# The first stage of a hybrid decoder layer: later load of x's second chunk, chunk 0's K tiles between conditioning pairs

## The chip, the cores and the metric

The kernel runs on one core of a Trainium2 chip. The metric is the device time of one execution in microseconds. The profile is of one execution of the same program; its times count from the start of the span, and the execution as a whole took a little longer than its span.

## The reference, cut to what matters

One layer (DEPTH is 1) is computed for 1024 prompt tokens and 8 decode tokens, 1032 columns in all, in float32.

```python
def rmsnorm(x, g):
    xf = x.astype(jnp.float32)
    y = xf * lax.rsqrt(jnp.mean(xf * xf, axis=-1, keepdims=True) + EPS)
    return (y * g).astype(x.dtype)

def layer(x, c, ...):
    mod = jax.nn.silu(c) @ w_ada + b_ada                 # (1024) x (1024, 6144), per sequence
    sh1, sc1, gt1, sh2, sc2, gt2 = jnp.split(mod[:, None, :], 6, axis=-1)
    h = rmsnorm(x, norm1_g) * (1.0 + sc1) + sh1
    proj = h @ w_in
    xr, gr, q, k, v, o, ig, fg, u = jnp.split(proj, _in_splits(), axis=-1)
    ...                                                  # RG-LRU, mLSTM and pool groups -> y_a, y_b, y_c
    x = x + gt1 * (jnp.concatenate([y_a, y_b, y_c], axis=-1) @ w_out)
    h2 = rmsnorm(x, norm2_g) * (1.0 + sc2) + sh2
    x = x + gt2 * (jnp.square(jax.nn.relu(h2 @ w_ff1)) @ w_ff2)
```

Before the first product of `h @ w_in` the kernel needs `sh1` and `sc1`, the first two sixths of `mod`, and the norm of x.

## The kernel before

**Data.** Features lie on partitions (8 K tiles of 128), tokens in the free dimension, in 3 chunks of 344 columns; the decode tokens are the last 8 of chunk 2. Every operand of a dense product is split into a high and a low part of type fp32r, and a product is three matmuls: high x high, low x high, high x low (`dense`). One K tile of one output tile over one chunk is three matmuls of 344 columns.

**The first stage.** SyncE loads x's first chunk, then `w_ada` in 512 KB halves through a ring of four buffers (`RAWW`, `load_raw`). A conditioning *pair* i gives tiles 2i and 2i+1 of `mod`, from two halves; pairs 0 to 3 are `sh1`, pairs 4 to 7 are `sc1`. TensorE multiplies a half in 8 instructions (`ADA:i:0`, `ADA:i:1`), ScalarE copies the result to `ADS` behind the second half, TensorE turns it and adds its four row groups up (`ADT:i`, 4 records in the trace), VectorE writes `MOD` (`ADM:i`; one more step for pairs 4 to 7). `raw_used` makes SyncE wait, before it loads half n, until TensorE has used half n - 4.

**The norm.** For each chunk ScalarE squares 8 K tiles of x and VectorE adds them up (`SQ:c:part`, 4 tiles each), with two buffers between them. TensorE sums over partitions (`NS:c`), ScalarE takes the root, VectorE the reciprocal. A *piece* `N:c:kt` is x times scale times reciprocal on VectorE, the shift, the high part on ScalarE and the low part on GpSimd. The shift is added by ScalarE for K tiles under `SHIFTED` (two passes, `hi_norm`), and by VectorE for the others (`normed`).

**Dense work.** `w_in` is cut into 17 units. Units 0 and 1 are loaded early into `WR` buffers of their own, unit 2 as well; `W:u` splits a unit's weights (high part on ScalarE, low part on GpSimd). `DK:u:c:k0:k1` multiplies K tiles k0 to k1 - 1 of unit u with chunk c, one at a time as pieces become ready; `D:u:c` is the whole product. `WV:j` splits a quarter of `w_v`, `V:t` computes V and the gates of 128 tokens (24 matmuls of 392 columns), which VectorE copies out.

**What sets the order.** The text `MIX_ORDER` is the program: each engine walks through it from the first word to the last and issues what of each word is its own, in that order. `SP_AFTER` says behind which half SyncE issues which other load. Engines meet only at semaphores. PSUM banks are given out by `bank_uses`.

```python
N_SP_RAW = 2 * len(ADA_START) + RAW
SP_AFTER = {3: ("x1",), 10: ("w1", "w0",), 16: ("wv",), 17: ("w2",), 18: ("x2",)}
N_EARLY_W = 3
```

Of the kernel before, what the change touches and what calls it, by code (L numbers as in the profile page):

```python
# [89 lines left out]


MIX_ORDER = """
ADA:0:0 ADA:0:1 SQ:0:0 ADA:4:0 ADA:4:1 SQ:0:1 SQ:1:0 ADT:0 ADM:0 ADA:1:0 SQ:1:1 ADA:1:1 ADT:4 ADM:4 NS:0
ADA:5:0 ADA:5:1 N:0:0 ADT:1 ADM:1 N:0:1 ADA:2:0 ADA:2:1 ADT:5 ADM:5 ADA:6:0 ADA:6:1 ADT:2 ADM:2 N:0:2 ADA:3:0 W:0
    ADA:3:1 ADT:6 N:0:3 W:1 ADM:6 ADA:7:0 ADA:7:1 ADT:3 N:0:4 N:0:5 ADM:3 ADT:7 ADM:7 N:0:6 N:0:7 NS:1
DK:0:0:0:6
WV:0 DK:1:0:0:6
DK:0:0:6:8
WV:1 WV:2 DK:1:0:6:8
ADA:8:0  # L100
D:0:0 WV:3
D:1:0 N:1:0 N:1:1 N:1:2 N:1:3 N:1:4 V:0 SQ:2:0 DK:0:1:0:1
DK:1:1:0:1
DK:0:1:1:2
N:1:5 DK:1:1:1:2
DK:0:1:2:3
N:1:6 N:1:7 DK:1:1:2:3
DK:0:1:3:4
DK:1:1:3:4
SQ:2:1 DK:0:1:4:5  # L110
DK:1:1:4:5
R:20 ADA:8:1 DK:0:1:5:6
V:1 DK:1:1:5:6
NS:2
ADT:8 DK:0:1:6:7
DK:1:1:6:7
DK:0:1:7:8
V:2 DK:1:1:7:8
D:0:1
D:1:1 N:2:8 N:2:0 R:21 N:2:1 N:2:2 N:2:3 N:2:4 N:2:5 N:2:6 V:3 V:4 ADM:8 DK:0:2:0:8  # L120
N:2:7 W:2 V:5
D:0:2 R:22 DK:1:2:0:8
ADA:9:0 ADA:9:1 R:23 V:6 V:7 W:3 V:8 R:25 ADT:9
D:1:2 ADM:9 ADA:10:0 G1 ADA:10:1
# [2758 lines left out]
```

## Time and profile before

| | |
|---|---|
| Median of 3 runs | 1188.4 us (1185.46 to 1189.35) |
| The profiled execution | 1188.24 us |
| Its span | 1186.4 us |
| Mean granted clock of TensorE | 0.986 |
| TensorE, busy | 1126.2 us, 95% of the span |
| VectorE, ScalarE, GpSimd, busy | 795.0, 472.8, 349.9 us |
| DMA | 109.85 MB |

The page's slices show TensorE nearly filled from the third slice on (a slice is 29.7 us); the first two are busy by 4 and 7 tenths, and there the DMA engines are busy by 8. The chain that ended last is 70% TensorE over the whole run. In the timeline a row gives its start, its length, the engine, the line, what is written from what, the count of instructions merged into it, and in brackets the idle time ahead of it with what ended it. A line number is that of the code that records the instruction: L2375 is a conditioning half, L2389 a turn, L2395 a sum of squares, L2404 to L2406 a K tile, L2431 to L2433 V. On VectorE L1760 adds squares, L1739 is the reciprocal, L1725 and L1729 are a piece's first and second instruction, L1714 and L1716 write MOD, L1774 is the low part of w_v. On ScalarE L1251 and L1252 are a piece's two passes, L1297 the eviction ahead of a turn; on GpSimd L1087 is a piece's low part and L1082 that of weights.

### The profile page before, as it was taken

To read this page: it belongs to the slowest core of one execution; us is meant where nothing else is said; L and a number is where in the kernel's file an instruction comes from. 1 tells how busy PE (TensorE), PEld (TensorE's weight loads), DVE (VectorE), ACT (ScalarE), POOL (GpSimd) and SP (SyncE) were. 2 spreads that over 40 slices of the span, in tenths; PEclk is the share of its full clock that TensorE was granted. 3 is DMA by queue.
4 is the path that set the end of the run, shared out by engine and by line. 5 is a ranking of instruction groups with operands and counts; after the bars stand their busy time and mean duration, and the time that the engine had idled before them with its cause. 6 is when DMAs were issued, how large, how long until landed. Compare 5 with 4: busy or idle time off the path is not lost.

```text
span 1186.4 us, 19681 instructions
## 1 busy us (share of the span) xinstructions
PE 1126.2 (95%) x7237; PEld 1075.9 (91%) x7237; DVE 795.0 (67%) x1319; ACT 472.8 (40%) x780; POOL 349.9 (29%) x275
## 2 busy tenths in 40 slices
PE   4799999999989999999999999999999999999997
PEld 2598988798879999899999999999999999999996
DVE  5561455578775434777678778787787787688646
ACT  5551355545456343641332332422432432423431
POOL 0442111101535267763032122122221231231252
PEclk9799999999989999999999999999999999999998
DMA  8812523556623722111111202101201102111104
GB/s 313 309 56 92 152 85 131 182 158 210 189 80 124 267 70 73 50 54 36 37 35 54 71 19 72 53 19 69 71 18 70 54 18 71 53 49 58 36 1 143
DMA packets 67845, 109.85 MB, mean 93 GB/s; under 512 B 6434, under 2 KB 42566, under 8 KB 67398
## 3 DMA queue, kind: packets, MB, share of 16 engines
q1 hardware_dynamic: 57574, 84.88, 21.6%
q10 hardware_dynamic: 10208, 24.12, 6.4%
q8 instruction: 41, 0.67, 0.2%
q14 instruction: 22, 0.18, 0.0%
HBM read 96.81 MB, written 12.18 MB: 92 GB/s over the span
## 4 chain that ended last, share of the span: by engine, by line
PE 70%; DVE 17%; ACT 4%; issue 3%; DMA 2%; POOL 1%; SPq 1%; DVEq 0%; ACTq 0%; POOLq 0%
PE D L2404 7%; PE D L2406 6%; PE D L2405 6%; PE D L2588 5%; PE D L2590 5%; PE D L2589 5%; PE X L2588 4%; PE X L2590 4%; PE X L2589 4%; PE X L2660 4%; PE X L2662 3%; PE X L2661 3%; PE D L2660 2%; PE D L2661 2%; PE D L2662 2%
## 5 line engine op out<-in xcount | busy, mean ns | idle before, releaser
L2404 PE MATMUL D<-H_hi,W_hi 128*128 128x344 f32 x472 | 158.8, 336 | 3.8 <-POOL H_lo L1087 3.1
L2406 PE MATMUL D<-H_hi,W_lo 128*128 128x344 f32 x472 | 152.7, 324 | 0.0
L2405 PE MATMUL D<-H_lo,W_hi 128*128 128x344 f32 x472 | 152.7, 323 | 0.0
L1087 POOL TENSOR_TENSOR Y_lo<-FU,Y_hi 128x344 fp32r<-128x344 f32 (+3 forms) x84 | 105.9, 1263 | 157.7 <-ACT Y_hi L1521 88.6
L1082 POOL TENSOR_TENSOR W_lo<-RAWW,W_hi 128x1024 fp32r<-128x1024 f32 x25 | 61.6, 2466 | 181.7 <-ACT W_hi L1234 181.4
L2404 PEld LDWEIGHTS D<-H_hi,W_hi 128*128 128x128 f32 x472 | 90.8, 192 | 11.9 <-issue 7.6
L1087 POOL TENSOR_TENSOR Y_lo<-EY,Y_hi 128x344 fp32r<-128x344 f32 (+1 forms) x24 | 35.4, 1474 | 220.6 <-ACT Y_hi L1521 143.3
L2405 PEld LDWEIGHTS D<-H_lo,W_hi 128*128 128x128 f32 x472 | 90.5, 192 | 0.9 <-issue 0.5
L2406 PEld LDWEIGHTS D<-H_hi,W_lo 128*128 128x128 f32 x472 | 90.4, 192 | 0.0
L2212 DVE SCALAR_TENSOR_TENSOR X<-X,MOD 128x344 f32<-128x344 f32 (+1 forms) x138 | 75.7, 567 | 9.2 <-PE X L2662 9.0
L2660 PE MATMUL X<-Y_hi,W_hi 128*128 128x344 f32 x252 | 80.7, 320 | 0.0
L2661 PE MATMUL X<-Y_lo,W_hi 128*128 128x344 f32 x252 | 80.6, 320 | 0.0
L2662 PE MATMUL X<-Y_hi,W_lo 128*128 128x344 f32 x252 | 80.5, 319 | 0.0
L2014 DVE SCALAR_TENSOR_TENSOR X<-D,MOD,X 128x344 f32<-128x344 f32 (+1 forms) x72 | 41.3, 573 | 45.4 <-PE D L2590 24.7
L2404 PE MATMUL D<-Y_hi,W_hi 128*128 128x344 f32 x192 | 62.1, 323 | 1.5 <-POOL W_lo L1082 1.5
L1087 POOL TENSOR_TENSOR Y_lo<-KEPT,Y_hi 128x344 fp32r<-128x344 f32 x24 | 26.4, 1099 | 124.1 <-ACT Y_hi L1521 124.1
L1099 POOL TENSOR_TENSOR SS<-SS,SQ 128x344 f32<-128x344 f32 x45 | 43.4, 964 | 65.9 <-ACT SQ L1430 40.4
L2406 PE MATMUL D<-Y_hi,W_lo 128*128 128x344 f32 x192 | 61.3, 320 | 0.0
L2405 PE MATMUL D<-Y_lo,W_hi 128*128 128x344 f32 x192 | 61.3, 319 | 0.0
L1556 ACT ACTIVATE W_hi<-RAWW 128x1024 fp32r<-128x1024 f32 x30 | 31.8, 1059 | 64.2 <-PE X L2662 55.5
L2375 PE MATMUL X<-RAWW,CTX 128*32 128x256 f32 x384 | 35.4, 456 | 19.6 <-DMA RAWW<-in_WADA 19.5
L2212 DVE SCALAR_TENSOR_TENSOR X<-D,MOD,X 128x344 f32<-128x344 f32 (+1 forms) x78 | 42.8, 568 | 16.4 <-PE D L2662 15.4
(416 smaller groups left out, 3443.4 us busy)
## 6 DMA issues: line engine op xcount, KB each, us to landing
RAWW<-in_W SPq DMA_DIRECT2D x76, 512.0 KB, 3.5
RAWW<-in_WADA ACTq DMA_DIRECT2D x28, 512.0 KB, 4.2
RAWW<-in_WADA SPq DMA_DIRECT2D x20, 512.0 KB, 8.0
RAWW<-in_W ACTq DMA_DIRECT2D x18, 512.0 KB, 3.7
X0T<-in_x SPq DMA_DIRECT2D x3, 1376.0 KB, 12.7
out_y<-OUTN SPq DMA_DIRECT2D x24, 172.0 KB
X<-in_x SPq DMA_DIRECT2D x8, 344.0 KB, 4.7
NM<-nm_d SPq DMA_DIRECT2D x8, 256.0 KB, 6.0
```

The source lines that it names most:

```text
L1082: nc.gpsimd.tensor_tensor(lo_v, RAWW[:, raw, :] if src is None else src[:], hi_v.bitcast(F32), ALU.subtract).then_inc(w_lo_ready, 1)
L1087: nc.gpsimd.tensor_tensor(lo_v, fu_v, hi_v.bitcast(F32), ALU.subtract).then_inc(lo_ready, 1)
L2212: V.scalar_tensor_tensor(out=X[:, m, c * CH:c * CH + w], in0=ps[:, 0:w], scalar=MOD[:, 5 * KT + m, 0:1], in1=X[:, m, c * CH:c * CH + w], o ...
L2404: T.matmul(out, w_h, hi[:, kt, a:b], start=(kt == 0), stop=False)
L2405: T.matmul(out, w_h, lo[:, kt, a:b], start=False, stop=False)
L2406: one = T.matmul(out, w_l, hi[:, kt, a:b], start=False, stop=(kt == KT - 1))
L2588: T.matmul(out, w_h, hi(kt), start=(kt == 0 and not onto), stop=False, skip_group_check=onto)
L2589: T.matmul(out, w_h, lo(kt), start=False, stop=False, skip_group_check=onto)
L2590: one = T.matmul(out, w_l, hi(kt), start=False, stop=(kt == n - 1), skip_group_check=onto)
L2660: T.matmul(bank[:, 0:CH], w_hi[:, a:a + P], h, start=(start and k == 0), stop=False, skip_group_check=onto)
L2661: T.matmul(bank[:, 0:CH], w_hi[:, a:a + P], l, start=False, stop=False, skip_group_check=onto)
L2662: one = T.matmul(bank[:, 0:CH], w_lo[:, a:a + P], h, start=False, stop=(stop and k == 1), skip_group_check=onto)
```

## The change

The loads of SyncE are ordered anew, the first seven lines of `MIX_ORDER` are written anew, the low parts of units 0 and 1 are computed on VectorE, and VectorE adds the shift for K tiles 4 to 7 of the first norm. The sum of squares of chunk 1 moves to another bank (X3).

```diff
-SP_AFTER = {3: ("x1",), 10: ("w1", "w0",), 16: ("wv",), 17: ("w2",), 18: ("x2",)}
+SP_AFTER = {7: ("w0", "w1"), 15: ("wv", "x1"), 17: ("x2",), 18: ("w2",)}
 N_EARLY_W = 3
+N_DVE_W = 2
...
-    ADA:3:1 ADT:6 N:0:3 W:1 ADM:6 ADA:7:0 ADA:7:1 ADT:3 N:0:4 N:0:5 ADM:3 ADT:7 ADM:7 N:0:6 N:0:7 NS:1
-DK:0:0:0:6
+ADA:5:0 ADA:5:1 ADT:5 ADM:5 W:0 N:0:2 W:1 N:0:3 ADA:2:0 DK:0:0:0:2 ADA:2:1 DK:1:0:0:2 ADT:2 ADM:2 ADA:6:0 DK:0:0:2:4 ADA:6:1
...
+D:1:0 SQ:1:0 SQ:1:1 V:0 NS:1 ADA:8:0 N:1:0 N:1:1 V:1 N:1:2 N:1:3 DK:0:1:0:1
...
-            add(s, ("X0", "X2", "X0")[s[1]])
+            add(s, ("X0", "X3", "X0")[s[1]])
...
-    SHIFTED = KT - 2
+    SHIFTED, SHIFTED_FIRST = KT - 2, KT // 2
...
-                    if s[1] < N_EARLY_W:
+                    if s[1] < N_DVE_W:
+                        pass
+                    elif s[1] < N_EARLY_W:
                         w_lo(s[1], None, s[1] % 2, WR[s[1]])
...
-                if kt >= SHIFTED:
+                if kt >= (SHIFTED if shift else SHIFTED_FIRST):
                     hi(n, hi_v, fu_v)
...
-                    if kt >= SHIFTED:
+                    if kt >= (SHIFTED if shift else SHIFTED_FIRST):
                         link(one)
                         one = V.tensor_scalar(v, v, MOD[:, shift + kt, 0:1], None, ALU.add)
...
+                elif k == "W" and s[1] < N_DVE_W:
+                    u = s[1]
+                    dve.wait_ge(w_hi_ready, u + 1)
+                    V.tensor_tensor(W_lo[:, u, :], WR[u][:], W_hi[:, u, :].bitcast(F32), ALU.subtract).then_inc(w_lo_ready, 1)
```

`shift` is 0 in the first norm and not 0 in the second, so the second norm keeps its rule.

SyncE's queue at the head, before (x4 and the like are instructions in a row; RAWW is a half, X0T a chunk of x):

```order
L802 DMA X0T_57<-in_x 128x8x344
L556 DMA RAWW_53<-in_WADA 128x2x512 x4
L802 DMA X0T_57<-in_x 128x8x344
L556 DMA RAWW_53<-in_WADA 128x2x512 x7
L822 DMA WR1_86<-in_W 128x1024
L822 DMA WR0_85<-in_W 128x1024
L556 DMA RAWW_53<-in_WADA 128x2x512 x6
L817 DMA WV_raw_97<-in_wv 128x3136
```

The same queue now:

```order
L799 DMA X0T_57<-in_x 128x8x344
L553 DMA RAWW_53<-in_WADA 128x2x512 x8
L819 DMA WR0_85<-in_W 128x1024
L819 DMA WR1_86<-in_W 128x1024
L553 DMA RAWW_53<-in_WADA 128x2x512 x8
L814 DMA WV_raw_97<-in_wv 128x3136
L799 DMA X0T_57<-in_x 128x8x344
```

The second load of x moved from behind four halves to behind all sixteen and w_v; the two units' weights moved forward by three halves.

TensorE behind the pair 1, before (X are conditioning banks, D0 and D1 the dense ones; 2 rows of SEL are a turn):

```order
L2375 MATMUL X4<-RAWW_53,CTX_135 32x256 x8
L2389 MATMUL X1<-SEL_139,ADS_138 128x9 x2
L2375 MATMUL X3<-RAWW_53,CTX_135 32x256 x8
L2389 MATMUL X1<-SEL_139,ADS_138 128x9 x2
L2375 MATMUL X4<-RAWW_53,CTX_135 32x256 x8
L2389 MATMUL X1<-SEL_139,ADS_138 128x9 x4
L2395 MATMUL X2<-SS_124,ONE_142 128x344
L2404 MATMUL D0<-H_hi_49,W_hi_54 128x344
```

TensorE at pair 2 now:

```order
L2378 MATMUL X3<-RAWW_53,CTX_135 32x256 x4
L2407 MATMUL D0<-H_hi_49,W_hi_54 128x344
L2408 MATMUL D0<-H_lo_50,W_hi_54 128x344
L2409 MATMUL D0<-H_hi_49,W_lo_55 128x344
...
L2378 MATMUL X3<-RAWW_53,CTX_135 32x256 x4
L2407 MATMUL D1<-H_hi_49,W_hi_54 128x344
...
L2392 MATMUL X1<-SEL_139,ADS_138 128x9 x2
```

Two K tiles of unit 0 stand between the two halves of pair 2, two of unit 1 between its second half and its turn; pairs 6 and 7 have the like, pair 3 has none.

VectorE around the same place, before:

```order
L1714 TENSOR_TENSOR MOD<-X,COLS 128x18
L1716 SCALAR_TENSOR_TENSOR MOD<-MOD,COLS 128x18
L1714 TENSOR_TENSOR MOD<-X,COLS 128x18
L1725 SCALAR_TENSOR_TENSOR FU<-X0T,MOD,X 128x344 x2
L1714 TENSOR_TENSOR MOD<-X,COLS 128x18
```

VectorE now:

```order
L1715 SCALAR_TENSOR_TENSOR MOD<-MOD,COLS 128x18
L1773 TENSOR_TENSOR W_lo<-WR_85,W_hi 128x1024
L1724 SCALAR_TENSOR_TENSOR FU<-X0T,MOD,X 128x344
L1773 TENSOR_TENSOR W_lo<-WR_86,W_hi 128x1024
L1724 SCALAR_TENSOR_TENSOR FU<-X0T,MOD,X 128x344
L1713 TENSOR_TENSOR MOD<-X,COLS 128x18 x2
```

The low parts of units 0 and 1 stand between the MOD steps of pairs 5 and 2, each ahead of a piece.

## Rows read from the trace of the kernel before

**Rows 1.** Waits: engine and line, releaser, total us, times, longest.

```profile
PE X L2375 <- DMA RAWW<-in_WADA: 19.5, 7, 10.0
```

**Rows 2.** Windows: length, busy us (x) by engine, granted clock, DMA share, GB/s.

```profile
39.00:42.00 3.00, 3.00 (x28) 1.48 (x20) 1.48 (x2) 2.76 (x6) 2.59 (x2) 0.50 0.78 254
...
51.00:54.00 3.00, 3.00 (x21) 3.00 (x21) 2.96 (x4) 0.12 (x1) 0.00 (x0) 1.00 1.07 386
```

**Rows 3.** Timeline of TensorE, 13 to 94 us.

```profile
13.97 1.08 PE L2375 MATMUL X<-RAWW,CTX 128*32 128x256 f32 x8 [0.28 <-DMA RAWW<-in_WADA]
...
24.15 1.94 PE L2375 MATMUL X<-RAWW,CTX 128*32 128x256 f32 x16
...
26.85 1.07 PE L2375 MATMUL X<-RAWW,CTX 128*32 128x256 f32 x16
...
44.05 0.99 PE L2389 MATMUL X<-SEL,ADS 128*128 128x9 f32 x4 [0.77 <-DVE MOD L1714]
44.89 1.50 PE L2395 MATMUL X<-SS,ONE 128*128 128x344 f32 x2
...
48.19 0.49 PE L2405 MATMUL D<-H_lo,W_hi 128*128 128x344 f32 x1
48.48 0.49 PE L2406 MATMUL D<-H_hi,W_lo 128*128 128x344 f32 x1
...
54.30 0.32 PE L2404 MATMUL D<-H_hi,W_hi 128*128 128x344 f32 x1
54.46 0.32 PE L2405 MATMUL D<-H_lo,W_hi 128*128 128x344 f32 x1
...
57.23 0.45 PE L2431 MATMUL X<-WV_hi,H_hi 128*128 128x392 f32 x1 [0.78 <-DVE WV_lo L1774]
...
61.57 0.32 PE L2404 MATMUL D<-H_hi,W_hi 128*128 128x344 f32 x1
...
66.38 0.64 PE L2375 MATMUL X<-RAWW,CTX 128*32 128x256 f32 x8
68.46 0.39 PE L2404 MATMUL D<-H_hi,W_hi 128*128 128x344 f32 x1 [1.43 <-POOL H_lo L1087]
...
93.05 0.42 PE L2404 MATMUL D<-H_hi,W_hi 128*128 128x344 f32 x1 [0.36 <-POOL H_lo L1087]
```

**Rows 4.** SyncE's transfers into RAWW (the first 60 us), then into WR: landing.

```profile
DMA to landing us min/median/max: 3.8/8.0/14.8
...
DMA to landing us min/median/max: 6.1/6.2/11.2
```

**Rows 5.** Groups by line, first 60 us: count, busy us, mean ns, idle before.

```profile
L1087 POOL TENSOR_TENSOR H_lo<-FU,H_hi 128x344 fp32r<-128x344 f32 x10 | 9.3, 940 | 45.1 <-ACT FU L1252 45.1
L1760 DVE TENSOR_TENSOR SS<-SS,SQ 128x344 f32<-128x344 f32 x16 | 8.3, 517 | 8.0 <-ACT SQ L1278 7.4
...
L1725 DVE SCALAR_TENSOR_TENSOR FU<-X0T,MOD,X 128x344 f32<-128x344 f32 x13 | 7.0, 569 | 0.9 <-POOL H_lo L1087 0.7
...
L1251 ACT ACTIVATE H_hi<-FU,MOD 128x344 fp32r<-128x344 f32 x9 | 5.2, 576 | 2.9 <-DVE FU L1725 2.9
...
L1739 DVE RECIPROCAL X<-SS 128x344 f32<-128x344 f32 x2 | 4.6, 2311 | 2.2 <-ACT SS L1257 2.2
...
L1774 DVE TENSOR_TENSOR WV_lo<-WV_raw,WV_hi 128x784 fp32r<-128x784 f32 x4 | 3.7, 972 | 2.2 <-ACT WV_hi L1282 2.2
...
L1297 ACT ACTIVATE ADS<-X 128x256 f32<-128x256 f32 x8 | 3.0, 380 | 15.9 <-PE X L2389 9.9 <-PE X L2375 6.0
```

**Rows 6.** Groups of VectorE over the whole run: splits of a later unit.

```profile
L2031 DVE TENSOR_TENSOR W_lo<-RAWW,W_hi 128x1024 fp32r<-128x1024 f32 x8 | 9.8, 1229 | 12.9 <-ACT W_hi L1234 12.9
```

**Rows 7.** Timelines of VectorE and of GpSimd, 40 to 41 us.

```profile
40.49 0.18 DVE L1714 TENSOR_TENSOR MOD<-X,COLS 128x18 f32<-128x18 f32 x1 [1.80 <-PE X L2389]
40.70 2.02 DVE L1716 SCALAR_TENSOR_TENSOR MOD<-MOD,COLS 128x18 f32<-128x18 f32 x1
...
40.32 2.36 POOL L1082 TENSOR_TENSOR W_lo<-WR,W_hi 128x1024 fp32r<-128x1024 f32 x1
```

More of the change, by code:

```diff
@@ L92 @@
 MIX_ORDER = """
-ADA:0:0 ADA:0:1 SQ:0:0 ADA:4:0 ADA:4:1 SQ:0:1 SQ:1:0 ADT:0 ADM:0 ADA:1:0 SQ:1:1 ADA:1:1 ADT:4 ADM:4 NS:0
-ADA:5:0 ADA:5:1 N:0:0 ADT:1 ADM:1 N:0:1 ADA:2:0 ADA:2:1 ADT:5 ADM:5 ADA:6:0 ADA:6:1 ADT:2 ADM:2 N:0:2 ADA:3:0 W:0
-    ADA:3:1 ADT:6 N:0:3 W:1 ADM:6 ADA:7:0 ADA:7:1 ADT:3 N:0:4 N:0:5 ADM:3 ADT:7 ADM:7 N:0:6 N:0:7 NS:1
-DK:0:0:0:6
[L97 to L100, printed above, removed]
+SQ:0:0 ADA:0:0 SQ:0:1 ADA:0:1 ADA:4:0 ADT:0 ADM:0 NS:0 ADA:4:1 ADT:4 ADM:4 ADA:1:0 N:0:0 ADA:1:1 N:0:1 ADT:1 ADM:1
+ADA:5:0 ADA:5:1 ADT:5 ADM:5 W:0 N:0:2 W:1 N:0:3 ADA:2:0 DK:0:0:0:2 ADA:2:1 DK:1:0:0:2 ADT:2 ADM:2 ADA:6:0 DK:0:0:2:4 ADA:6:1
+    ADT:6 ADM:6 DK:1:0:2:4 N:0:4 ADA:3:0 N:0:5 ADA:3:1 ADT:3 ADM:3 ADA:7:0 DK:0:0:4:6 ADA:7:1 ADT:7 ADM:7 DK:1:0:4:6 N:0:6 N:0:7
+WV:0 WV:1 DK:0:0:6:8
+WV:2 DK:1:0:6:8
 D:0:0 WV:3
-D:1:0 N:1:0 N:1:1 N:1:2 N:1:3 N:1:4 V:0 SQ:2:0 DK:0:1:0:1
+D:1:0 SQ:1:0 SQ:1:1 V:0 NS:1 ADA:8:0 N:1:0 N:1:1 V:1 N:1:2 N:1:3 DK:0:1:0:1
 DK:1:1:0:1
[L104 to L108, printed above, removed]
+N:1:4 DK:0:1:1:2
+DK:1:1:1:2
+N:1:5 DK:0:1:2:3
+DK:1:1:2:3
+N:1:6 DK:0:1:3:4
 DK:1:1:3:4
-SQ:2:1 DK:0:1:4:5
+N:1:7 DK:0:1:4:5
 DK:1:1:4:5
 R:20 ADA:8:1 DK:0:1:5:6
-V:1 DK:1:1:5:6
-NS:2
+SQ:2:0 DK:1:1:5:6
 ADT:8 DK:0:1:6:7
 DK:1:1:6:7
-DK:0:1:7:8
-V:2 DK:1:1:7:8
+SQ:2:1 DK:0:1:7:8
+DK:1:1:7:8
 D:0:1
-D:1:1 N:2:8 N:2:0 R:21 N:2:1 N:2:2 N:2:3 N:2:4 N:2:5 N:2:6 V:3 V:4 ADM:8 DK:0:2:0:8
-N:2:7 W:2 V:5
+D:1:1 V:2 NS:2 N:2:8 N:2:0 R:21 N:2:1 N:2:2 V:3 N:2:3 N:2:4 N:2:5 N:2:6 V:4 ADM:8 N:2:7 DK:0:2:0:8
+W:2 V:5
 D:0:2 R:22 DK:1:2:0:8
```

## The prediction, made before any run of the changed kernel

> **What bounds the kernel now.** I read the waits of TensorE first. Over the whole run its longest wait is for transfers of w_ada: 19.5 us in 7 waits, of which the first is the 10.0 us until any weight has landed [rows 1]. All of it lies before 60 us. TensorE waits little for the rest of the run, so a microsecond won or lost at the head moves everything behind it. I therefore compare the moment at which TensorE has reached the same point of the work.
>
> The windows of the head come next [rows 2]. From 39 to 42 us the granted clock was 0.50, the lower level (1.2 GHz), although TensorE was busy for all of it, with conditioning halves and their turns; from 51 us it was 1.00. The DMA engines moved 386 GB/s from 51 to 54 us, but 254 from 39 to 42: they are not always the bound of the head. The timeline gives the price of a level [rows 3]: dense matmuls follow each other by 0.29 us at the lower clock and by 0.16 at the higher one, so a K tile (three) costs 0.87 or 0.48 us; a conditioning half (8 matmuls) costs 1.08 or 0.64. A turn costs 0.99 at the lower clock, taken as 0.5 at the higher.
>
> The last turn of the sixteen halves ends at 45.0 (44.05 + 0.99); behind chunk 1's sum of squares chunk 0 is multiplied, V of the first 128 tokens starts at 57.23 after a 0.78 us wait, and chunk 1 starts at 61.57; then come waits of 1.43 us at 68.46 and 0.36 at 93.05 [rows 3]. V of 128 tokens costs 4.3 us (61.57 - 57.23), 4.2 of it streaming. The point that I compare is "V:0 and V:1 done, chunk 1 beginning, later waits included": 61.57 + 4.2 + 1.43 + 0.36 = **67.6 us** before.
>
> **The change, part by part.**
>
> *x's second chunk out of the way.* It is 1376 KB. Halves of 512 KB land 1.36 us apart (1.08 of work and 0.28 of waiting at 13.97) [rows 3], so it takes 3.7 us of the stream, and the fifth half can land at 15.3 instead of 19.1. That is no gain by itself: only four halves fit in the ring, and a new one is issued when TensorE has used the one four back. A re-issue into a drained queue lands 3.8 us later at best [rows 4].
>
> *First three pairs.* In the new order pair 0's evicted sums stand on ScalarE behind all eight squares. x lands at about 8.6 (one spacing before the first half at 10.0); eight squares and adds, each add 0.52 and a handover [rows 5], end at 13.4. TensorE: three halves until 13.7, turn to 14.8, sum of squares 1.35 (a start-to-start share of the 1.50 at 44.89) [rows 3] to 16.2, fourth half to 17.3. Each turn now stands directly behind its own pair, so eviction (0.38) [rows 5] and two handovers, 0.46 us, are waited for each time. Turn 18.7, two halves 20.9, 0.7 wait behind the two ScalarE passes of the first K tile, turn 22.5, two halves 24.7, wait and turn **26.1**. The eighth half was re-issued at 17.3 and lands at 21.1 where the bare stream would have brought it at 19.4: 1.7 us of stream lost. Behind it stand w0 and w1. A WR load needed 6.1 us or more to land, against 3.8 for the quickest half [rows 4], though both have 512 KB; bounds are 1.36 us, a half's spacing, and 1.36 + 2.3. I take 2.4 us of stream each, near the middle. The ninth half then lands at 21.1 + 4.8 + 1.36 = 27.3, a wait of 1.1.
>
> *Pairs 2, 6, 3, 7 with ten K tiles between them.* From 27.3 to the last turn there are 8 halves, 4 turns and 10 of the 16 K tiles. At the lower clock: 8.6 + 4.0 + 8.7 = 21.3, plus 2.1 of waits (0.6 for the split of w1, 0.1, three evictions of 0.46) = **50.7**. At the higher clock: 5.1 + 2.0 + 4.8 = 11.9, plus 5.4 of waits (2.3 for w1's split, 0.9 for the third turn's sums queued behind an N piece on ScalarE, 1.3 for a half that could be issued late, two evictions) = **44.5**. So the end of this stretch is no longer set by the DMA stream alone; it depends on TensorE's clock.
>
> *Splits of w0 and w1 on VectorE.* 1.23 us each there [rows 6] instead of 2.36 on GpSimd [rows 7]. They are inside the waits above. Queued behind w1's split is the fourth N piece, behind that the sums of pair 2.
> In the trace the 18-element VectorE step at 40.70 took 2.02 us beside GpSimd's W_lo, begun at 40.32, where the step of the same size ahead of it took 0.18 [rows 7]. The Trainium skill (SBUF — State Buffer, Who interferes with whom) says that a VectorE instruction with two SBUF inputs and a GpSimd instruction that reads SBUF exclude each other and the second waits in full. The trace agrees; by that rule a split on VectorE could wait for one H_lo (0.94) or hold one back, at most 0.9 us more than my sum, which has GpSimd idle when both splits start.
>
> *The shift of K tiles 4 to 7 on VectorE.* A piece cost VectorE one instruction (0.57, of which 0.51 from start to start) and ScalarE two (0.96 from start to start, 0.58 and 0.57 alone) [rows 5]; now VectorE has a second and a handover, about 0.98, and ScalarE 0.49, in each chunk. A K tile of two units is 0.95 us of TensorE, so the pieces just keep up; nothing is won in chunk 0, where pieces wait for sums.
>
> *From the last turn to chunk 1.* Two steps of MOD 0.4, two N pieces 2.0, then ScalarE's first part of w_v (0.85) and four VectorE parts at 0.97 [rows 5], handovers: V:0 starts 7.7 us after the last turn (the six K tiles left fit inside). V:0 4.2, chunk 1's sum 0.8, one half 0.6, V:1 4.2. The squares of chunk 1 (4.4 us, behind w_v's last part on VectorE) end inside V:0; behind the sum stand root 0.55, reciprocal 2.31, the first piece 0.57 + 0.96 + 0.94 [rows 5]: that is 0.75 longer than the half and V:1. Together 7.7 + 4.2 + 0.8 + 0.6 + 4.2 + 0.75 = **18.3**. Later: 0.7 in chunk 1 and 1.3 in chunk 2, whose last pieces now cost VectorE 0.98. My handovers are rounded down; the same count over the rows of before is 0.9 short over this stage, most of it on steps that the new order exposes more often, so I add 0.9.
>
> *Sum.* Lower clock throughout: 50.7 + 18.3 + 2.0 + 0.9 = 71.9, that is +4.3 on 67.6. Higher clock from 27 us: 44.5 + 18.3 + 2.0 + 0.9 = 65.7, that is -1.9. Which one? Before, it went up near 27 us, behind a sum of squares, two halves and a turn without a gap: the 16 matmuls of two halves at 24.15 took 1.94 us, the 16 at 26.85 took 1.07 [rows 3]. It stayed down from 39 to 42 us with halves and turns alone [rows 2], and rose again between 48.48 and 54.30, inside chunk 0's dense matmuls [rows 3]. The new order puts two bursts of 1.7 us between halves at 28 to 34 us, nearer to the case that raised it. I take it as rising after the second burst, which costs 0.6 on top: **-1.3 us**. The profiled execution took 1188.2 us (span 1186.4), the median is 1188.4; so 1187.0 us.
>
> **The rivals.**
> *The clock stays low.* The bursts are too thin among turns and waits, and the ten K tiles cost 0.87 each on a path that was DMA's. For it: 39 to 42 us of before, where a busy TensorE kept 0.50 [rows 2]. Against it: there was no dense work in it. Place: TensorE between 28 and 50 us; it decides against the kernel once the rise comes later than about 40 us (half of the 6.2 us between the two sums). Price +4.3: **1192.6 us**, slower.
> The Trainium skill (TensorE: Matmul & The Clock Gate, What's actually happening) has it that the low clock is the default and activity releases it; by this a mixed stretch can go either way, and the rows above are all that tells here.
>
> *The quick case.* The clock is up from the first sum of squares on: the halves and turns between 17 and 27 us save 1.9 us more, and the new order has no handovers longer than I counted, 0.9. Then -4.1: **1184.2 us**, faster. For it: the first sum of squares now stands closer to halves. Against it: halves still wait for transfers there.
>
> *The stream decides after all.* If w0 and w1 slow the stream more, or the late re-issues add up, the last half comes late and w_v and x's second chunk with it. In my walk the second chunk lands near 48 to 50 us and its squares start near 52 to 58, behind w_v's splits; there are 4 us or more of cover. Above that each microsecond counts in full. I give it little.
>
> **How the numbers follow.** The forecast case, clock rising between 27 and 38 us, 0.55, gives 1185.5 to 1189; low clock 0.2, 1192.6; quick case 0.2, 1184.2; late stream 0.05, above 1190. About 0.3%, 3.6 us, is what a measurement of this kernel tells from no change. The quick case passes that bound in most of its chance, the forecast case in a small part: faster 0.26; slower 0.19 from the low clock and the late stream; same 0.55. The range reaches from a little below the quick case to the low-clock case: 1183.3 to 1192.6.
>
> **What would show it.** Right: the last turn near 45 to 46 us with ten K tiles behind it, dense matmuls before 45 us mostly 0.16 us apart, V:0 7.7 us after the last turn, chunk 1 beginning at 63 to 65 us. Wrong: clock 0.50 until 50 us (low-clock case); the ninth half before 26 us (w0 and w1 cheaper); V:0 waiting for w_v's transfer instead of its splits; a wait of over 1 us at the start of chunk 1 for the second chunk of x; or a difference that arises behind 120 us, where I expect none.

## The result, and the profile after

The changed kernel took 1192.4 us (median of 14 runs, 1188.4 to 1195.7) where the kernel before, on the same chip, took 1187.9 (14 runs): a ratio of 1.0034, with a 95% interval from 1.0020 to 1.0048. It is slower by some 4 us. Eight further runs of the unaltered file gave 1.0020 (1.0000 to 1.0039). The forecast was 1187.0 us; the time is near that of the rival "the clock stays low", 1192.6.

The profiled execution of the changed kernel took 1193.7 us, with a span of 1191.9 and a mean granted clock of 0.983 (before: 1188.2, 1186.4, 0.986). Its windows (length, busy us and count by engine, granted clock, DMA share, GB/s) answer to [rows 2]:

```profile
30.00:33.00 3.00, 2.09 (x15) 1.13 (x14) 1.71 (x2) 1.22 (x3) 0.62 (x1) 1.00 0.58 205
33.00:36.00 3.00, 2.37 (x15) 1.44 (x15) 0.18 (x1) 0.67 (x2) 0.91 (x1) 0.67 0.33 126
36.00:39.00 3.00, 2.44 (x17) 1.58 (x15) 0.00 (x0) 0.38 (x1) 0.00 (x0) 0.76 0.48 175
39.00:42.00 3.00, 2.33 (x25) 1.47 (x24) 2.18 (x6) 0.49 (x1) 0.28 (x1) 1.00 0.79 267
42.00:45.00 3.00, 2.12 (x16) 1.69 (x17) 0.21 (x2) 0.76 (x2) 1.67 (x2) 0.88 1.02 429
45.00:48.00 3.00, 2.44 (x15) 1.19 (x13) 0.00 (x0) 0.38 (x1) 0.00 (x0) 0.50 0.98 363
...
57.00:60.00 3.00, 3.00 (x11) 3.00 (x11) 2.66 (x6) 2.42 (x5) 0.00 (x0) 0.50 1.01 372
60.00:63.00 3.00, 3.00 (x15) 3.00 (x14) 1.09 (x3) 0.52 (x2) 0.00 (x0) 0.78 0.17 51
```

Until 28 us a half still takes 1.08 us, the duration at the lower level, whatever the windows there show (more on this at the end); the clock is high from 30 us, falls between 33 and 39, rises, and falls again near 44; from 45 to 60 us every window has 0.50. Before, it was low from 33.5 to 50.6 us, and its fall came in TensorE's longest wait for a transfer but the first (5.38 us, in the timeline of the kernel before):

```profile
35.28 1.08 PE L2375 MATMUL X<-RAWW,CTX 128*32 128x256 f32 x8 [5.38 <-DMA RAWW<-in_WADA]
```

Behind this half TensorE waited for no transfer any more, so the halves and turns up to 45.0 us ran almost back to back at the lower level, but for 0.77 us of waiting for a step of MOD. What that cost the kernel before is measured in e5.

TensorE's waits of the changed kernel in the first 66 us (engine and line, releaser, total us, times, longest) answer to [rows 1]:

```profile
PE X L2378 <- DMA RAWW<-in_WADA: 11.5, 4, 10.4
PE X L2392 <- ACT ADS L1296: 5.4, 7, 1.5
PE D L2407 <- POOL H_lo L1084: 1.5, 1, 1.5
PE D L2407 <- DVE W_lo L1773: 0.9, 1, 0.9
PE X L2434 <- DVE WV_lo L1777: 0.6, 1, 0.6
```

The wait for transfers fell from 19.5 us to 11.5, and all but 1.1 us of what is left is the first half. In its place stand 5.4 us for ScalarE's evictions of sums, one before almost every turn. TensorE's timeline (start, us, the group, and in brackets the wait ahead of it and its releaser) answers to [rows 3]:

```profile
25.27 1.02 PE L2392 MATMUL X<-SEL,ADS 128*128 128x9 f32 x4 [0.56 <-ACT ADS L1296]
27.00 1.08 PE L2378 MATMUL X<-RAWW,CTX 128*32 128x256 f32 x8 [0.71 <-DMA RAWW<-in_WADA]
...
31.89 0.43 PE L2407 MATMUL D<-H_hi,W_hi 128*128 128x344 f32 x1 [0.91 <-DVE W_lo L1773]
...
45.81 1.08 PE L2378 MATMUL X<-RAWW,CTX 128*32 128x256 f32 x8
47.46 1.03 PE L2392 MATMUL X<-SEL,ADS 128*128 128x9 f32 x4 [0.56 <-ACT ADS L1296]
...
51.86 0.62 PE L2407 MATMUL D<-H_hi,W_hi 128*128 128x344 f32 x1 [1.46 <-POOL H_lo L1084]
...
56.22 0.70 PE L2434 MATMUL X<-WV_hi,H_hi 128*128 128x392 f32 x1 [0.58 <-DVE WV_lo L1777]
56.71 0.53 PE L2435 MATMUL X<-WV_lo,H_hi 128*128 128x392 f32 x1
57.04 0.53 PE L2436 MATMUL X<-WV_hi,H_lo 128*128 128x392 f32 x1
...
62.90 0.74 PE L2398 MATMUL X<-SS,ONE 128*128 128x344 f32 x2
63.56 0.64 PE L2378 MATMUL X<-RAWW,CTX 128*32 128x256 f32 x8
...
69.47 0.39 PE L2407 MATMUL D<-H_hi,W_hi 128*128 128x344 f32 x1 [0.80 <-POOL H_lo L1084]
```

The last turn ends at 48.5 us instead of 45.0, with ten K tiles of chunk 0 already done. V of the first 128 tokens starts at 56.22, a microsecond before it did before, but takes 6.7 us (to 62.90) where it took 4.3: its matmuls follow each other by 0.33 us instead of 0.18.

To compare kernels I take one point that all of them have: VectorE's copy of the last V, of 8 tokens, which ends the first stage. VectorE's timeline of the kernel before, then of the changed one:

```profile
115.82 0.55 DVE L1785 COPY VS<-X 8x384 f32<-8x384 f32 x1 [3.47 <-PE X L2433]
```

```profile
120.11 0.55 DVE L1788 COPY VS<-X 8x384 f32<-8x384 f32 x1 [3.47 <-PE X L2436]
```

That is +4.29 us of the 5.4 between the two profiled times. From this copy to the end of the span the kernel before took 1070.6 us and the changed one 1071.8; in the other profiles here it is 1068.3 to 1071.6, but for e1 (1075.4, taken up at the end). There are short falls of the clock between 235 and 280 us and near 345 that differ from execution to execution. So most of the loss arises before 120 us.

### The profile page after: what moved, and what is told of

It reads as the page before. It is cut to its first block, busy times and chain, and to the rows that moved or that the text cites. A ratio compares the mean times of both kernels' runs of the same rounds, so it can differ in the third digit from the quotient of the medians.

```text
span 1191.9 us, 19690 instructions
## 1 busy us (share of the span) xinstructions
PE 1134.0 (95%) x7237; PEld 1080.9 (91%) x7237; DVE 797.1 (67%) x1327; ACT 470.2 (39%) x774; POOL 345.4 (29%) x273
## 4 chain that ended last, share of the span: by engine, by line
PE 71%; DVE 16%; ACT 4%; issue 3%; DMA 2%; POOL 2%; SPq 1%; DVEq 0%; ACTq 0%; POOLq 0%
PE D L2407 7%; PE D L2409 6%; PE D L2408 6%; PE D L2591 5%; PE D L2593 5%; PE D L2592 5%; PE X L2591 4%; PE X L2593 4%; PE X L2592 4%; PE X L2663 3%; PE X L2665 3%; PE X L2664 3%; PE D L2663 2%; PE D L2664 2%; PE D L2665 2%
## 5 line engine op out<-in xcount | busy, mean ns | idle before, releaser
L2215 DVE SCALAR_TENSOR_TENSOR X<-D,MOD,X 128x344 f32<-128x344 f32 (+1 forms) x78 | 42.8, 568 | 16.4 <-PE D L2665 15.4
L1084 POOL TENSOR_TENSOR H_lo<-FU,H_hi 128x344 fp32r<-128x344 f32 (+2 forms) x33 | 30.4, 936 | 74.6 <-ACT FU L1251 47.6
## 6 DMA issues: line engine op xcount, KB each, us to landing
X0T<-in_x SPq DMA_DIRECT2D x3, 1376.0 KB, 11.5
```

What stands on the lines that cost most here:

```text
L1084: nc.gpsimd.tensor_tensor(lo_v, fu_v, hi_v.bitcast(F32), ALU.subtract).then_inc(lo_ready, 1)
L2215: V.scalar_tensor_tensor(out=X[:, m, c * CH:c * CH + w], in0=ps[:, 0:w], scalar=MOD[:, 5 * KT + m, 0:1], in1=X[:, m, c * CH:c * CH + w], o ...
```

## The experiments

"Stage end" below is the start of that copy, less the 115.82 of before. It comes from one execution of each kernel, and those of e2, e3 and e5 were the shortest of their series; a median is over the whole series. The first half alone starts anywhere from 9.87 to 10.66 us in the profiles named here (9.99 before, 10.37 changed, 9.95 in e1), so a few tenths between two stage ends say nothing. "F:n" is n matmuls of 128x344 into a bank that nobody reads; they fill waits of TensorE and do no other work.

**e1: the changed kernel with its waits filled.**

```
-  ... ADA:2:0 DK:0:0:0:2 ADA:2:1 DK:1:0:0:2 ADT:2 ... ADA:6:1
-      ADT:6 ... ADA:3:1 ADT:3 ... ADA:7:1 ADT:7 ...
-  WV:0 WV:1 DK:0:0:6:8
-  D:1:0 SQ:1:0 SQ:1:1 V:0 ...
+  ... ADA:2:0 DK:0:0:0:2 ADA:2:1 F:5 DK:1:0:0:2 F:3 ADT:2 ... ADA:6:1
+      F:3 ADT:6 ... ADA:3:1 F:8 ADT:3 ... ADA:7:1 F:3 ADT:7 ...
+  WV:0 WV:1 F:8 DK:0:0:6:8
+  D:1:0 SQ:1:0 SQ:1:1 F:3 V:0 ...
```

> The changed kernel with 33 extra matmuls of 344 columns into a bank that is still unused, put where TensorE waited between 31 and 56 us (5 and 3 around pair 2's tiles, 3 before turn 6, 8 before turn 3, 3 before turn 7, 8 before K tile 6, 3 before V:0); all results stay as they are. Theory C (the clock): the changed order leaves TensorE with too many waits, the clock falls at 44 us and stays low until 61, in V:0 too. Then these matmuls keep it up: V:0 takes 4.3 us instead of 6.7, chunk 1 begins at 64 to 66 us instead of 69.5, and the time is 3 to 5 us under the changed kernel's, about that of the kernel before. Theory L (the chain of latencies): the loss is that each turn waits for its own pair's eviction and that ring buffers are issued late; the last turn then stays at 48 us, and with 33 extra matmuls the time is the changed kernel's or up to 2 us more.

Measured: 1189.4 us (12 runs), ratio 1.0002 (0.9985 to 1.0019), 3 us less than the changed kernel; the two intervals, this and 1.0020 to 1.0048, don't overlap, though this one does overlap that of the repeated changed kernel (1.0000 to 1.0039). TensorE's timeline, then a window:

```profile
44.60 0.61 PE L2392 MATMUL X<-SEL,ADS 128*128 128x9 f32 x4
...
52.87 0.45 PE L2434 MATMUL X<-WV_hi,H_hi 128*128 128x392 f32 x1 [1.33 <-DVE WV_lo L1777]
...
53.50 0.34 PE L2434 MATMUL X<-WV_hi,H_hi 128*128 128x392 f32 x1
```

```profile
45.00:48.00 3.00, 2.52 (x16) 2.23 (x16) 2.21 (x6) 0.79 (x2) 0.64 (x1) 1.00 1.09 397
```

The windows from 33 to 66 us all have a granted clock of 1.00, and the halves from 34.0 us on take 0.64 us each. The last turn ends at 45.2 instead of 48.5, V's matmuls follow by 0.18 us again, and the stage end is at -1.06. Work that computes nothing, 33 matmuls of it, brought the stage end 5.35 us forward. The order, the transfers and the splits are those of the changed kernel, and 0.42 us is the earlier first half; what is left is, as far as these traces show, the clock's. Against the second profile of the unaltered kernel (e11, below), in which the clock stayed up for longer, the same work brought 2.2 us: what fillers are worth depends on the course that they are compared with. The stage end is also where the forecast's sum for a clock that rises and stays had put it, -1.3.

**e2: the changed kernel with the ten K tiles behind the last turn again.**

```
-  (DK:0:0:0:2 DK:1:0:0:2 DK:0:0:2:4 DK:1:0:2:4 DK:0:0:4:6 DK:1:0:4:6 from among halves and turns)
-  WV:0 WV:1 DK:0:0:6:8
+  DK:0:0:0:6 DK:1:0:0:6 WV:0 WV:1 DK:0:0:6:8
```

> The changed kernel, but the K tiles of chunk 0 are all multiplied behind the last turn, as before the change; loads, turns, splits and V as in the changed kernel. Theory C: the last turn comes some 4 us earlier than 48.5, since 10 K tiles at mostly the lower clock are gone from ahead of it; then 12 K tiles in a row raise the clock before V:0, which takes 4.3 us; chunk 1 begins at 65 to 67 us, the time is 1 to 3 us under the changed kernel's. Theory L: the last turn gains what the tiles cost, but the tiles cost it again behind; time as the changed kernel within 1 us.

Measured: 1191.9 us (12 runs), ratio 1.0034 (1.0021 to 1.0048); stage end +1.26. In the median it is no better than the changed kernel, so K tiles among halves are not by themselves what costs. The profiled execution, the shortest of the twelve (1189.5), ends the stage 3 us before the changed kernel's first profile and level with its second: all sixteen K tiles stand together, the clock rises among them near 47.5 us, and V:0 takes 4.5 us. The loss has another source as well, which shows without the tiles:

```profile
32.31 1.02 PE L2390 MATMUL X<-SEL,ADS 128*128 128x9 f32 x4 [4.72 <-ACT ADS L1294]
...
35.76 1.02 PE L2390 MATMUL X<-SEL,ADS 128*128 128x9 f32 x4 [0.56 <-ACT ADS L1294]
...
40.38 1.03 PE L2390 MATMUL X<-SEL,ADS 128*128 128x9 f32 x4 [1.73 <-ACT ADS L1294]
```

TensorE waits 4.72 us for the sums of pair 2, which are queued on ScalarE behind the splits of w0 and w1 and two N pieces. All the evictions together cost it 10.9 us in the first 66. The last turn ends at 44.9, where before's ended (45.0): what the late second chunk of x gave to the stream, the turns behind their own pairs took. All of this ran at the lower level: from 21.4 us to the last turn every two halves took 1.94 us and every turn 1.02. Only from 13.7 to 18.3 us was the clock up here, with 0.64 us for a half.

**e3: the order of pairs, turns and K tiles of before; only x's second chunk late, with what follows from it.**

```
   (of the changed kernel)
-  SQ:0:0 ADA:0:0 SQ:0:1 ADA:0:1 ADA:4:0 ADT:0 ADM:0 NS:0 ... (its first stage up to DK:1:0:6:8)
+  ADA:0:0 ADA:0:1 SQ:0:0 ADA:4:0 ADA:4:1 SQ:0:1 ADT:0 ... (that of before, without SQ:1:0, SQ:1:1, NS:1)
```

> One part alone: x's second chunk late, w_v and the two units' weights as in the changed kernel, and all words of chunk 1 and of V as there; but pairs, turns, pieces and K tiles of chunk 0 in the order of the kernel before. Both theories: last turn near 43 to 45 us. Theory C: TensorE has the dense stretch of before, V:0 at the higher clock, chunk 1 begins at 66 to 67.5, the time within 1.5 us of the kernel before. If the late chunk itself is the cost (theory X: its squares and reciprocal stand behind V:0 and are waited for), the time is 3 us or more over the kernel before whatever the clock.

Measured: 1188.9 us (12 runs), ratio 1.0011 (0.9997 to 1.0026), last turn at 42.8, chunk 1 beginning at 64.6, stage end -0.59. So the load moved back, V of 256 tokens moved ahead, the splits on VectorE and the four shifts make no difference that is measured. The last turn does come 2.3 us earlier than before. It starts here, then V:0:

```profile
41.77 0.99 PE L2394 MATMUL X<-SEL,ADS 128*128 128x9 f32 x4 [1.26 <-DVE MOD L1715]
...
53.38 0.44 PE L2436 MATMUL X<-WV_hi,H_hi 128*128 128x392 f32 x1 [1.35 <-DVE WV_lo L1779]
```

Turns of about 1 us and halves of 1.08 say that this kernel ran at the lower level from its first half up to its last turn; its dense matmuls follow by 0.16 us from 46.2 us on. So the clock doesn't make e2 the slower one up to there: 2.1 us at the last turn (44.9 and 42.8) and 1.85 at the stage end are the price of the order of turns, pieces and splits (0.2 of it is the earlier first half of e3), with 10.9 us of waits for evictions in e2 where e3 has 4.5 for steps of MOD. V:0 starts at 53.38, and 1.35 us of that is a wait for the last split of w_v, which stands on ScalarE behind the eviction of chunk 0.

**e4: the changed kernel, x's second chunk issued early, behind the fourth half.**

```
-SP_AFTER = {7: ("w0", "w1"), 15: ("wv", "x1"), 17: ("x2",), 18: ("w2",)}
+SP_AFTER = {3: ("x1",), 7: ("w0", "w1"), 15: ("wv",), 17: ("x2",), 18: ("w2",)}
```

> The changed kernel with x's second chunk loaded behind the fourth half, as before the change; nothing else differs. If the stream bounds the first stage, every half from the fifth on lands 3.7 us later and the time is 3 to 4 us over the changed kernel's. Under C and L TensorE, its waits and its clock bound it: half of that or less, 0 to 2 us more, because the ring drained anyway at 18 and between 33 and 40 us.

Measured: 1192.8 us (8 runs), ratio 1.0037 (1.0015 to 1.0060), last turn at 48.3, stage end +2.53, ahead of the changed kernel's +4.29 because here the clock was up again when V:0 started. The transfer that the change is named after can be put back without a measurable difference in the median. With this order the stream doesn't set the head any more, so freeing it gains nothing, and the rival "the stream decides" falls.

**e5: the kernel before with its waits filled.**

```
-  ADA:6:0 ADA:6:1 ADT:2 ... ADA:7:0 ADA:7:1 ADT:3 N:0:4 N:0:5 ADM:3 ADT:7
+  ADA:6:0 F:24 ADA:6:1 ADT:2 ... ADA:7:0 ADA:7:1 F:2 ADT:3 N:0:4 N:0:5 ADM:3 F:4 ADT:7
```

> The kernel before, whose order is untouched, with 30 matmuls of 128x344 into a bank that nobody reads, put where TensorE waits between 30 and 44 us: 24 of them into its longest wait (5.38 us, for a half of w_ada), 2 and 4 before the last two turns. Clock theory (the low clock from 34 to 50.6 us lies on the path of the kernel before too): sum of squares, the 36 K-tile matmuls that took 0.29 us each, and the turns behind 43 us run at the high clock, V of the first 128 tokens starts 2 to 3 us earlier than the 57.23 of before, the last V of the first stage is copied near 113 us instead of 115.8, and the time is about 0.2% shorter. Rival (the low clock is covered there, and w_v's splits on ScalarE and VectorE set V's start): V starts within 1 us of 57.2 and the time does not change.

Measured: 1188.9 us (10 runs), ratio 1.0009 (0.9990 to 1.0027). The clock was up by 37 us, V:0 started at 56.01, and the stage end is -1.22.

```profile
47.85 0.43 PE L2404 MATMUL D<-H_hi,W_hi 128*128 128x344 f32 x1 [0.95 <-POOL H_lo L1087]
...
48.84 0.42 PE L2404 MATMUL D<-H_hi,W_hi 128*128 128x344 f32 x1 [0.24 <-POOL H_lo L1087]
...
56.01 0.45 PE L2431 MATMUL X<-WV_hi,H_hi 128*128 128x392 f32 x1 [1.14 <-DVE WV_lo L1774]
```

My 2 to 3 us were too many. The faster K tiles run into the splits of H (1.2 us of waits), and V into w_v's splits. The kernel before had a cover for most of the low clock; filled waits are worth 1.2 us there against 5.35 in the changed kernel. With filled waits the two kernels end the stage within 0.16 us of each other (114.60 here, 114.76 in e1), so what lies between them without fillers is put down to the clock: 4.29 us in the first profiles, 0.7 in the second ones (below).

**e7: fillers around V:0 only.** 8 ahead of K tiles 6 and 7, 3 ahead of V:0, as in the last two lines of e1's edit.

> The changed kernel with 11 filling matmuls only: 8 ahead of K tiles 6 and 7 of chunk 0, 3 ahead of the first V; none between the pairs. It splits the gain of e1 (5.35 us at the last V of the first stage) between the two places. Clock theory: the last turn stays near 48.5 us, but the eight fill the wait behind it, so the clock is up when V starts: V takes 4.3 us instead of 6.7 and the last V is copied near 117.7 instead of 120.1; time about 0.15% above before. If what the clock does at V is settled by the thin work between the pairs, the eight don't raise it: V takes 6.7 us again and nothing changes.

Measured: 1190.1 us (10 runs), ratio 1.0021 (1.0002 to 1.0040). The last turn is as in the changed kernel (47.54 to 48.6), but

```profile
56.25 0.44 PE L2434 MATMUL X<-WV_hi,H_hi 128*128 128x392 f32 x1 [1.33 <-DVE WV_lo L1777]
...
60.75 0.84 PE L2398 MATMUL X<-SS,ONE 128*128 128x344 f32 x2
```

V takes 4.5 us instead of 6.7, and the stage end is 118.14, 1.97 before the changed kernel's. So of e1's 5.35 us some two come from the clock at V:0; the other 3.4 are the clock between the pairs and the 0.42 us of the first half.

**e8: each turn behind the first half of the next pair.**

```
-  ... ADA:0:1 ADA:4:0 ADT:0 ADM:0 NS:0 ADA:4:1 ADT:4 ADM:4 ADA:1:0 N:0:0 ADA:1:1 N:0:1 ADT:1 ADM:1
+  ... ADA:0:1 ADA:4:0 ADT:0 ADM:0 NS:0 ADA:4:1 ADA:1:0 ADT:4 ADM:4 N:0:0 ADA:1:1 N:0:1 ADA:5:0 ADT:1 ADM:1
   (and so on for pairs 5, 2, 6 and 3)
```

> The changed kernel with each turn moved behind the first half of the next pair, K tiles where they were. Rival to the clock (what the change lost is handover time: TensorE waits 5.6 us in 8 waits for ScalarE's evictions of sums before turns that stand directly behind their pair): these waits fall under 2 us, the last turn ends 2 to 4 us before 48.5, and the time is 0.2 to 0.3% shorter than the changed kernel's. Clock theory: the waits go, but the work between 34 and 61 us is as thin as before, the clock stays at its low level over the last turns and the first V, and V still takes 6 us or more; the gain is then at most 2 us.

Measured: 1191.5 us (10 runs), ratio 1.0031 (1.0012 to 1.0050), last turn at 48.6, V:0 6.1 us, stage end +3.83.

```profile
PE X L2378 <- DMA RAWW<-in_WADA: 14.5, 6, 10.4
PE X L2392 <- ACT ADS L1296: 4.1, 3, 2.6
PE D L2407 <- POOL H_lo L1084: 3.4, 1, 3.4
```

Of seven waits for evictions three are left, but they are longer. Transfers are waited for 3 us more, probably because the new order takes halves from the ring one place earlier, and K tile 6 3.4 us instead of 1.5. A handover that is hidden in one place came back in another. This version can't say what the handovers alone are worth: it never got rid of them.

**e11 and e12: the changed kernel and the kernel before once more, unaltered.**

> The changed kernel once more, unaltered, to see how much of its course repeats. Clock theory: the clock falls again around 34 and 44 us, as in its first profile, and is low over the last turns and at least the start of the first V; last turn at 46.5 to 48.5 us, the last V copied 2 to 5 us later than before's 115.8. If the first profile was an unlucky execution, the last turn comes at 45 us, V takes 4.3 us, and the last V is copied near 115.

> The kernel before once more, unaltered. Clock theory: low clock from about 33 to 50 us as in its first profile, in which TensorE waits for w_ada anyway, so the last V of the first stage is again copied within 1 us of 115.8. If the moments at which the clock moves are free within an execution, its rise may come up to a few us earlier or later in the K tiles, which moves the last V by up to 2 us.

The changed kernel took another course. Its windows, then TensorE's timeline:

```profile
33.00:36.00 3.00, 3.00 (x23) 2.38 (x21) 0.18 (x1) 0.94 (x3) 0.91 (x1) 1.00 0.52 175
36.00:39.00 3.00, 2.44 (x20) 1.55 (x19) 0.48 (x3) 0.38 (x1) 0.00 (x0) 1.00 0.60 185
...
48.00:51.00 3.00, 1.90 (x7) 1.90 (x8) 1.70 (x3) 2.73 (x4) 1.83 (x2) 0.50 1.06 385
51.00:54.00 3.00, 2.42 (x9) 1.98 (x8) 2.55 (x4) 2.29 (x5) 0.00 (x0) 0.50 1.08 381
```

```profile
45.11 0.61 PE L2392 MATMUL X<-SEL,ADS 128*128 128x9 f32 x4 [0.56 <-ACT ADS L1296]
...
49.10 0.62 PE L2407 MATMUL D<-H_hi,W_hi 128*128 128x344 f32 x1 [2.32 <-POOL H_lo L1084]
...
53.46 0.69 PE L2434 MATMUL X<-WV_hi,H_hi 128*128 128x392 f32 x1 [0.58 <-DVE WV_lo L1777]
...
59.75 0.74 PE L2398 MATMUL X<-SS,ONE 128*128 128x344 f32 x2
```

This time the clock rose near 33.6 us, inside the second burst of K tiles, and stayed up to the last turn, which ended at 45.7: the forecast's case, with its numbers. But it fell right behind, in the 2.3 us wait for K tile 6, and V:0 took 6.3 us again. Stage end +1.17. The kernel before gave +0.43, with low clock from about 30 us to 49.9 instead of 33.5 to 50.6. So before's head is worth the same in both of its executions (115.8 and 116.2), while the changed kernel's moved by 3.1 us (120.1 and 117.0) with the course of the clock. A second profile of each was needed to see this.

**e6, e9 and e10: looking for a version that gains.** All three start from e3. e6 has 17 fillers before 42 us, and w_v's splits and chunk 1's squares put ahead; e9 puts the split of w1 behind the step of MOD that a turn waits for; e10 is e9 without fillers.

```
   e6, against e3
+    F:5 ADA:3:1 ADT:6 N:0:3 W:1 ADM:6 ADA:7:0 ADA:7:1 F:5 ADT:3 N:0:4 N:0:5 ADM:3 F:7 ADT:7 ADM:7 WV:0 WV:1 N:0:6 N:0:7
+WV:2 WV:3 DK:1:0:0:6
+SQ:1:0 DK:1:0:6:8
+D:0:0 SQ:1:1
   e9, against e6
+    ADA:3:1 ADT:6 N:0:3 ADM:6 W:1 ADA:7:0 F:5 ADA:7:1 F:3 ADT:3 N:0:4 N:0:5 ADM:3 F:5 ADT:7 ADM:7 WV:0 WV:1 N:0:6 N:0:7
```

> The kernel of e3 (before's order of pairs, turns and K tiles, second chunk of x late) with two things more: 17 filling matmuls in TensorE's waits before 42 us, and w_v's splits and the squares of chunk 1 put ahead, so that no split of w_v stands behind an eviction of chunk 0. In e3 V of the first 128 tokens waited 1.35 us for the last split of w_v. Clock theory: V starts near 50.5 instead of 53.4 us, chunk 1 begins near 61.5 instead of 64.6, the last V is copied near 112 us, 3.8 us earlier than before, and the time is 1184 to 1186, about 0.3% shorter than before. If the early splits only move the wait (pieces of K tiles 6 and 7 late), V starts near 52 and the time is within 0.2% of before.

> The kernel of e6 with the split of w1 put behind the modulation step of the pair before it on VectorE (in e6 that step stood from 36.6 to 40.0 behind the split, and the turn behind it started at 40.7 although its halves were done at 39.2), and the fillers moved to suit (13 instead of 17). If the turns are what still holds the first stage: the last turn starts near 40.5 instead of 43.3 us, V of the first 128 tokens near 49.5, chunk 1 near 59.5 (e6: 62.8), the last V of the first stage is copied near 110.5 (e6: 113.5, before: 115.8), and the time is 1183 to 1185, 0.3 to 0.4% shorter than before. Rival: the clock stays low for longer, because less is done before 42 us, and the K tiles behind the last turn run at 0.29 us a matmul: then V starts no earlier than 51 and the last V is copied at 112.5 or later.

> The kernel of e9 without any filling matmul. Clock theory: the clock rises 3 to 5 us later, inside the K tiles of chunk 0 (in e3, without fillers, it rose near 46 us), some 20 to 25 matmuls cost 0.29 instead of 0.16 us, and V starts 2 to 3 us later than in e9 (near 52), the last V is copied 2 to 3 us later, time 0.2% more than e9. Rival: the splits of w_v bound V's start anyway (49.5), and the two kernels differ by less than 1 us at the last V.

| | stage end | median us (runs) | ratio, 95% |
|---|---|---|---|
| e6 | -2.37 | 1186.5 (10) | 0.9985 (0.9963 to 1.0007) |
| e9 | -3.25 | 1185.4 (12) | 0.9993 (0.9977 to 1.0008) |
| e10 | -2.22 | 1186.3 (10) | 0.9991 (0.9978 to 1.0003) |

The stage ends earlier in all three, by less than I expected. In e9 the clock was at its lower level until about 44 us in spite of fillers (K tile matmuls of 0.49 us up to there), the last turn started at 42.10 instead of 40.5, and V:0 at 51.1 instead of 49.5. What the fillers buy there, e9 against e10, is 1 us, near the rival's "less than 1". Two or three microseconds at the stage end are 0.2 to 0.3% of the time; no interval excludes 1, so none of these is shown to be faster than the kernel before. Against the changed kernel the case is clearer: their intervals end below the 1.0020 at which that of its 14 runs begins, though they overlap that of its eight repeated runs, which begins at 1.0000. In the series of e9 and e10 its repeat had a median of 1189.9 us, 3.6 to 4.5 us above theirs.

## Why the prediction was wrong

**The step that failed is the choice of the clock.** "I take it as rising after the second burst" held in neither execution as it was meant, namely up to chunk 1. In the first profile the clock was up from 30 us, fell in the thin stretches at 34 and at 44 and stayed low until 61.4; in e11 it rose at 33.6, as taken, but fell behind the last turn. The rows I argued from showed when it had risen; I had none that showed what keeps it up, and gave that question no term; V:0 stood at 4.2 us in every case, and took 6.7 and 6.3. Of 33 to 39 and 45 to 48 us the windows say that TensorE was busy 2.4 of 3 us, in short groups with a wait before each turn.

**The sums for the two cases were good, one of them by luck.** With the clock held up (e1) the stage end came at -1.06, forecast -1.3. With it low, +4.29, forecast +4.3. But in the low case two errors cancel: the last turn came at 48.5, not 50.7, since part of the stretch from 27 us was at the higher level; and V:0, which I left at 4.2 us in both cases, took 6.7. e7 prices that at 2 us. The first sum has a slip of 0.1 (27.3 + 11.9 + 5.4 is 44.6, not 44.5), which changes nothing. The right form of the rival would have had the clock fall a second time behind the last turn.

**The other terms, one by one.** Ninth half: forecast 27.3 after a wait of 1.1, measured 27.00 after 0.71. Evictions: 0.46 us each, measured 0.56 for four of the seven, 0.63 and 0.97 for two, and 1.55 for the turn of pair 3, whose sums stand behind N pieces; 5.4 us in all in the first 66. Splits on VectorE: priced 1.23 [rows 6], measured

```profile
30.61 1.23 DVE L1773 TENSOR_TENSOR W_lo<-WR,W_hi 128x1024 fp32r<-128x1024 f32 x1 [2.07 <-ACT W_hi L1233]
...
39.60 0.18 DVE L1715 SCALAR_TENSOR_TENSOR MOD<-MOD,COLS 128x18 f32<-128x18 f32 x1
```

The second row answers to the 2.02 us step of [rows 7]: with no W_lo on GpSimd beside it, it takes 0.18. The rule that the prediction cites from the Trainium skill (SBUF — State Buffer, Who interferes with whom) fits this step and that of [rows 7]; the microsecond that it allowed for wasn't seen. From the last turn to V:0: forecast 7.7 us, measured 7.7 in both profiles (48.5 to 56.22, 45.7 to 53.46) and in e1 (45.2 to 52.87). This term did not depend on the clock, because the splits of w_v set it. From V:0's end to chunk 1: forecast 6.35, measured 6.57. Behind the start of chunk 1: forecast 2.9 where before had 1.79 of waits, so +1.1; measured +0.6 (50.64 us to the stage end, against 115.82 - 61.57 - 4.24 = 50.01 before).

**Of the rivals,** "the clock stays low" was the nearest, in its place and nearly in its price; I gave it 0.2 although [rows 2] showed three microseconds of unbroken work that did not raise the clock. That row should have weighed more than the single rise near 27 us, all the more since the order lost in both of its profiles, and in neither was the clock up to the end of V:0. The "quick case" did not come about in the changed kernel: halves took 1.08 us until 28 us in both profiles. Its clock did come in e2, where a half took 0.64 us from 14.9 us on, and was gone again by 20.4 us, behind a wait of 2.17 us for an eviction. "The stream decides" fell with e4. Behind 120 us, where I expected no difference, the changed kernel's first profile is 1.2 us longer than before's and its second 0.7 us shorter, inside what the profiles of one kernel differ by (before: 1070.6 and 1068.3).

**What stays open.** How much of the loss is the clock's on average. In the first profile it accounts for nearly all of +4.29 us (with the waits filled the stage end is at -1.06, and that of before at -1.22); in the second V:0 alone took 2 us more than at the higher level, against a stage end of +1.17. Two profiles don't say how often each course comes. e8 was to price the handovers within the changed order, and traded one wait for another; only e2 against e3 prices the order without the clock, at about 2 us. The medians of e1 and e5 (+0.9 and +1.2 us against the same chip's before) lie 2 us above their stage ends (-1.06 and -1.22). e5's profiled execution was the shortest of its ten, 1186.2 where the median is 1188.9, and the others weren't profiled. Of e1's, which was long (1192.1), the record tells more. Its windows behind the first stage:

```profile
230.00:250.00 20.00, 17.14 (x118) 15.27 (x117) 9.74 (x20) 7.48 (x11) 2.35 (x1) 0.83 0.75 220
265.00:285.00 20.00, 18.46 (x118) 17.65 (x117) 16.68 (x31) 11.42 (x14) 2.35 (x1) 0.83 0.56 179
```

From 340 to 360 us it is 0.83 too. The kernel before has 0.91, 1.00 and 0.83 in the same three windows. By an estimate from these levels (the share of the clock that is missing, times 20 us) that is 10.2 us against 5.2, and from stage end to the end of the span e1 took 1075.4 us against 1070.6. So the later falls of the clock account for that execution. Whether the fillers of the first stage have a part in them isn't known.

## What to carry to other kernels

Where the clock changes the price of an order, write the sum for each stretch and ask of each what keeps the clock up in it, not only what raises it; a thin stretch just ahead of long matmuls is one of the expensive ones (2 us at V:0, e7). Moving work into the waits of an engine that a transfer bounds pays only if no new handovers are put on the path with it: here 8 us less waiting for transfers turned into 5.4 us of waiting for evictions, more low clock, and a loss. Profile both kernels twice before reading one stage's difference as the change's.
